# Matmul operands stored as pairs of 64-byte pieces, and activations shifted by 128 bytes

## The reference, cut to what matters

```python
def swiglu(x, wi, wo):
    gate, up = jnp.split(x @ wi, 2, axis=-1)      # wi 1024 x 5632
    return (jax.nn.silu(gate) * up) @ wo          # wo 2816 x 1024
...
for li in range(DEPTH):                           # DEPTH = 2
    h = h + 0.5 * swiglu(rms_norm(h, ffn1_norm[li]), ffn1_wi[li], ffn1_wo[li])
    hn = rms_norm(h, mix_norm[li])
    mix = gla_pool_mixer(hn, ...) if li % 2 == 0 else dsa_mixer(hn, ...)
    h = h + mix
    h = h + 0.5 * swiglu(rms_norm(h, ffn2_norm[li]), ffn2_wi[li], ffn2_wo[li])
```

## Time and profile before

| what | value |
|---|---|
| median of 2 runs | 1460.0 us (1459.95 to 1460.05) |
| the profiled execution's own time | 1459.98 us |
| its span, first to last instruction | 1458.1 us |
| PE busy | 1451.5 us, 7822 matmuls |
| DVE busy, ACT busy | 1002.2 us (69%), 777.7 us (53%) |
| moved from memory | 183 GB/s on average |
| TensorE clock granted | 1.0 throughout |

### The profile page before, as it was taken

One profiled execution on the slowest core, in us unless ns is written; L12 is line 12 of the kernel. 1 busy time (PEld: TensorE's weight loads), 2 busy tenths in 40 slices (PEclk: granted clock), 3 DMA queues, 4 the chain that ended last, 5 costly groups with the idle time before them and its releaser, 6 DMA issues.

```text
span 1458.1 us, 18627 instructions
## 1 busy us (share of the span) xinstructions
PE 1451.5 (100%) x7822; PEld 1250.3 (86%) x7822; DVE 1002.2 (69%) x1216; ACT 777.7 (53%) x971; POOL 87.1 (6%) x113
## 2 busy tenths in 40 slices
PE   9999999999999999999999999999999999999999
PEld 7888888888888888888888888888888888888887
DVE  6876466777755877459877764787646987687753
ACT  6654355655534555345665544565436876465542
POOL 0000003000000000006100000000000800000000
PEclk9999999999999999999999999999999999999999
DMA  9855563556556555545465556465556543566552
GB/s 328 277 176 185 159 204 116 167 180 201 178 184 200 190 181 195 185 141 172 149 200 188 185 177 206 154 223 182 188 173 217 188 145 118 173 196 201 179 188 72
DMA packets 205620, 266.82 MB, mean 183 GB/s; under 512 B 6944, under 2 KB 148880, under 8 KB 205280
## 3 DMA queue, kind: packets, MB, share of 16 engines
q1 hardware_dynamic: 204320, 261.23, 54.7%
q0 software_dynamic: 1072, 4.35, 0.8%
q10 hardware_dynamic: 144, 0.05, 0.0%
HBM read 264.56 MB, written 1.05 MB: 182 GB/s over the span
## 4 chain that ended last, share of the span: by engine, by line
PE 93%; DVE 3%; ACT 1%; DMA 1%; issue 0%; SPq 0%; DVEq 0%; ACTq 0%
PE ps L631 31%; PE ps L638 17%; PE ps L563 14%; PE ps L565 13%; PE ps L564 13%; PE ps L616 1%; DMA raw<-in_ffn_wi 1%; DVE wlo L1656 1%; PE ps L741 1%; PE ps L836 1%; PE ps L774 1%; DVE d_i L2049 0%; ACT whi L1217 0%; DVE d_m L2045 0%; DVE d_i L2073 0%
## 5 line engine op out<-in xcount | busy, mean ns | idle before, releaser
L1656 DVE TENSOR_TENSOR wlo<-raw,whi 128x2048 fp32r<-128x2048 f32 (+5 forms) x275 | 567.3, 2068 | 259.1 <-ACT whi L1217 258.9
L1217 ACT CAST whi<-raw 128x2048 fp32r<-128x2048 f32 (+5 forms) x275 | 474.0, 1729 | 223.0 <-PE ps L565 218.5
L631 PE MATMUL ps<-xt,whi 128*128 128x512 f32 x2112 | 501.7, 391 | 0.8 <-DVE xt L2249 0.7
L631 PEld LDWEIGHTS ps<-xt,whi 128*128 128x128 f32 x2112 | 389.3, 188 | 78.0 <-DVE xt L2249 1.5
L638 PEld LDWEIGHTS ps<-xt,wlo 128*128 128x128 f32 x2112 | 267.1, 191 | 8.2
L638 PE MATMUL ps<-xt,wlo 128*128 128x256 f32 x2112 | 269.6, 283 | 0.0
L563 PE MATMUL ps<-whi,xt 128*128 128x512 f32 (+4 forms) x304 | 112.7, 371 | 0.0
L565 PE MATMUL ps<-whi,xt 128*128 128x512 f32 (+4 forms) x304 | 109.7, 361 | 0.0
L564 PE MATMUL ps<-wlo,xt 128*128 128x512 f32 (+4 forms) x304 | 109.5, 360 | 0.0
L563 PEld LDWEIGHTS ps<-whi,xt 128*128 128x128 f32 x304 | 57.3, 189 | 9.2 <-issue 1.0
L565 PEld LDWEIGHTS ps<-whi,xt 128*128 128x128 f32 x304 | 57.2, 188 | 8.5
(11 more groups left out here) (422 smaller groups left out, 1884.3 us busy)
## 6 DMA issues: line engine op xcount, KB each, us to landing
raw<-in_ffn_wi SPq DMA_DIRECT2D x85, 1024.0 KB, 5.0
raw<-in_ffn_wo SPq DMA_DIRECT2D x40, 1024.0 KB, 4.9
raw<-in_ffn_w_gate SPq DMA_DIRECT2D x22, 1024.0 KB, 5.1
raw<-in_ffn_w_up SPq DMA_DIRECT2D x22, 1024.0 KB, 5.1
raw<-in_ffn_w_down SPq DMA_DIRECT2D x20, 1024.0 KB, 4.9
raw<-in_w_in SPq DMA_DIRECT2D x14, 1024.0 KB, 5.1
raw<-in_even_w_in SPq DMA_DIRECT2D x6, 1024.0 KB, 5.2
raw<-in_ffn_wo SPq DMA_DIRECT2D x8, 512.0 KB, 3.8
```

The costliest lines, as they stand in the source:

```text
L631: return e.matmul(Pair(job.name).ap[:, b, :], whi[:, v % SPLIT, 256 * j + 128 * b:256 * j + 128 * b + 128], XS[:, j, :, :].rearrange("p h ...
L1217: e.copy(whi[0:n, v % SPLIT, c], raw[0:n, v % RAW, c]).then_inc(s_hi.mark(*[(v, j) for j in js]), 1)
L1656: e.tensor_tensor(wlo[0:n, v % SPLIT, c], raw[0:n, v % RAW, c], whi[0:n, v % SPLIT, c].bitcast(F32), ALU.subtract).then_inc(s_lo.mark(*[(v ...
```

## The change

**Moving operands in pairs of pieces.** A moving row is no longer stored in the order in which it is read. The place it lies in is cut into two halves (for `xt` the 256 elements of the first and of the second 1024 bytes of a row of 512, for a weight block the first and second 4096 bytes of its slot), and the row is read as 16 elements (64 bytes) from the first half, 16 from the second, the next 16 from the first, and so on. The matmul's moving operand becomes a pattern of three dimensions, while its result still goes to PSUM as one unbroken row. The producers (ACT's casts, DVE's subtractions) write in the same pattern, from sources in plain order. This holds for all 4224 matmuls of `wide` and `two_wide`, and for all of `steps` and `by_tiles` but the 144 whose width is no multiple of 32 (272, 324, 360): 6954 of 7098 F32R matmuls in all, 4674 with 512 columns and 2280 with 256. Stationary operands stay unbroken.

**A shift of 128 bytes.** `xt`, `yt` and `ht` get 32 elements more. Their data now starts at an odd multiple of 128 bytes (`xt` at byte 107648, `yt` at 124032, `a1ht` at 164224), while `whi` and `wlo` stay at multiples of 256.

```diff
+class Paired(Turned):
+    def __init__(self, XS):
+        self.XS = XS
+    def moving(self, kt, q0, q1):
+        return self.XS[:, kt, :].rearrange("p (h q i) -> p q h i", h=2, i=16)[:, q0:q1]
+    def parts(self, kt, n):
+        return self.moving(kt, 0, 8)[0:n], self.moving(kt, 8, 16)[0:n]
+    def same(self, ap):
+        return ap.rearrange("p (q h i) -> p q h i", h=2, i=16)
...
-        self.hT = Turned(sb(self.name + "ht_hi", [128, 22, 256], F32R), sb(self.name + "ht_lo", [128, 22, 256], F32R))
+        room = sb(self.name + "ht", [128, 2 * 22 * 256 + 32], F32R)[:, 32:].rearrange("p (h k t) -> p h k t", h=2, k=22)
+        self.hT = Turned(room[:, 0], room[:, 1])
...
-        XS = sb("xt", [128, 8, 2, 256], F32R)
-        XT = Turned(XS[:, :, 0, :], XS[:, :, 1, :])
-        YT = Turned(sb("yt_hi", [128, 8, 256], F32R), sb("yt_lo", [128, 8, 256], F32R))
+        XS = sb("xt", [128, 4096 + 32], F32R)[:, 32:].rearrange("p (k t) -> p k t", k=8)
+        XT = Turned(XS[:, :, 0:256], XS[:, :, 256:512])
+        XP = Paired(XS)
+        yt_room = sb("yt", [128, 4096 + 32], F32R)[:, 0:4096].rearrange("p (h k t) -> p h k t", h=2, k=8)
+        YT = Turned(yt_room[:, 0], yt_room[:, 1])
...
+        def kept(w, v, n, a, b):
+            job, i = plan[v]
+            if job.blocks[0][1] == 8 or job.width % 32:
+                return w[0:n, v % SPLIT, a:b]
+            return w[0:n, v % SPLIT, :].rearrange("p (h q i) -> p q h i", h=2, i=16)[:, a // 32:b // 32]
+        def as_kept(ap, v):
+            ...
+            return ap.rearrange("p (q h i) -> p q h i", h=2, i=16)
...
-                    hi_w, lo_w = (w[0:n, v % SPLIT, j * wd:(j + 1) * wd] for w in (whi, wlo))
+                    hi_w, lo_w = (kept(w, v, n, j * wd, (j + 1) * wd) for w in (whi, wlo))
...
-                                    XS[:, j, :, :].rearrange("p h t -> p (h t)"), start=j == 0, stop=stop)
+                                    XP.moving(j, 0, 16), start=j == 0, stop=stop)
...
-                                    XS[:, j, 0, :], start=False, stop=stop)
+                                    XP.moving(j, 0, 8), start=False, stop=stop)
...
-                e.copy(whi[0:n, v % SPLIT, c], raw[0:n, v % RAW, c]).then_inc(s_hi.mark(*[(v, j) for j in js]), 1)
+                e.copy(kept(whi, v, n, c.start, c.stop), as_kept(raw[0:n, v % RAW, c], v)).then_inc(s_hi.mark(*[(v, j) for j in js]), 1)
...
-                e.tensor_tensor(wlo[0:n, v % SPLIT, c], raw[0:n, v % RAW, c], whi[0:n, v % SPLIT, c].bitcast(F32),
+                e.tensor_tensor(kept(wlo, v, n, c.start, c.stop), as_kept(raw[0:n, v % RAW, c], v), kept(whi, v, n, c.start, c.stop).bitcast(F32),
...
+                        elif act is XP:
+                            for r in range(2):
+                                if r:
+                                    t.then_inc(s_dve.mark(), 1)
+                                t = e.scalar_tensor_tensor(l[:, :, r, :], src[:, :, r, :], gains(i)[0:n, :], h[:, :, r, :].bitcast(F32), ALU.mult, ALU.subtract)
```

More of the change, by code:

```diff
@@ L137, in __init__, with parts, same @@
         self.hi, self.lo = hi, lo
+    def parts(self, kt, n):
+        return self.hi[0:n, kt, :], self.lo[0:n, kt, :]
+    def same(self, ap):
+        return ap
+class Paired(Turned):
[3 more added lines that the diff above has]
+        return self.XS[:, kt, :].rearrange("p (h q i) -> p q h i", h=2, i=16)[:, q0:q1]
+    def parts(self, kt, n):
+        return self.moving(kt, 0, 8)[0:n], self.moving(kt, 8, 16)[0:n]
+    def same(self, ap):
+        return ap.rearrange("p (q h i) -> p q h i", h=2, i=16)
 class Job:
@@ L249, in program @@
         wi1, wo1, wi2, wo2 = (T[n] for n in ("ffn1_wi", "ffn1_wo", "ffn2_wi", "ffn2_wo"))
-        a1 = Ffn("a1", "in", wi1[0], 0, wi1[0], FF, wo1[0], XT)
-        a2 = Ffn("a2", "gla", wi2[0], 0, wi2[0], FF, wo2[0], XT)
-        b1 = Ffn("b1", "a2", wi1[1], 0, wi1[1], FF, wo1[1], XT)
-        b2 = Ffn("b2", "dsa", wi2[1], 0, wi2[1], FF, wo2[1], XT)
-        c1 = Ffn("c1", "b2", T["ffn1_w_gate_2"][0], 0, T["ffn1_w_up_2"][0], 0, T["ffn1_w_down_2"][0], XT)
-        c2 = Ffn("c2", "mla", T["ffn2_w_gate_2"][0], 0, T["ffn2_w_up_2"][0], 0, T["ffn2_w_down_2"][0], XT)
+        a1 = Ffn("a1", "in", wi1[0], 0, wi1[0], FF, wo1[0],XP)
+        a2 = Ffn("a2", "gla", wi2[0], 0, wi2[0], FF, wo2[0],XP)
+        b1 = Ffn("b1", "a2", wi1[1], 0, wi1[1], FF, wo1[1],XP)
+        b2 = Ffn("b2", "dsa", wi2[1], 0, wi2[1], FF, wo2[1],XP)
+        c1 = Ffn("c1", "b2", T["ffn1_w_gate_2"][0], 0, T["ffn1_w_up_2"][0], 0, T["ffn1_w_down_2"][0],XP)
+        c2 = Ffn("c2", "mla", T["ffn2_w_gate_2"][0], 0, T["ffn2_w_up_2"][0], 0, T["ffn2_w_down_2"][0],XP)
         ga, gk, gu, gv, gg = col_jobs("gla", T["even_w_in"][0], D,
@@ L597, in by_tiles @@
                         q.wait_ge(*s_lo[v, j])
-                        hi_w, lo_w = (w[:, v % SPLIT, j * wd:(j + 1) * wd] for w in (whi, wlo))
+                        hi_w, lo_w = (kept(w, v, 128, j * wd, (j + 1) * wd) for w in (whi, wlo))
                         h, l = (a[:, kt, 128 * tt:128 * tt + 128] for a in (job.act.hi, job.act.lo))
@@ L1229, in turned @@
                         n = rows[i]
-                        t = e.mul(act.hi[0:n, kt0 + i, :], pair.flat[0:n, 256 * i:256 * i + 256], 1.0 if gains is None else gains(i)[0:n, :])
+                        t = e.mul(act.parts(kt0 + i, n)[0], act.same(pair.flat[0:n, 256 * i:256 * i + 256]), 1.0 if gains is None else gains(i)[0:n, :])
                     t.then_inc(s_act.mark((name, "hi", b)), 1)
@@ L1234, in turn_x @@
                 q.wait_ge(*s_dve["gains"])
-                turned(("xt", x, n), XT, 4 * n, lambda i: gains_of[x](4 * n + i))
+                turned(("xt", x, n), XT if x in ("a1", "b1", "c1") else XP, 4 * n, lambda i: gains_of[x](4 * n + i))
             def squares(x, n):
@@ L1613, in x_high @@
                 q.wait_ge(*s_xt[min(j // 2, 2)]["x"])
-                e.mul(XT.hi[:, j, :], XR[:, j, :], gain("f1", j)).then_inc(s_act.mark(("x0", j)), 1)
+                e.mul(XP.parts(j, 128)[0], XP.same(XR[:, j, :]), gain("f1", j)).then_inc(s_act.mark(("x0", j)), 1)
             x_high(0)
@@ L1665, in turned @@
                         n = rows[i]
-                        src, h, l = pair.flat[0:n, 256 * i:256 * i + 256], act.hi[0:n, kt0 + i, :], act.lo[0:n, kt0 + i, :]
+                        src, (h, l) = act.same(pair.flat[0:n, 256 * i:256 * i + 256]), act.parts(kt0 + i, n)
                         if gains is None:
                             t = e.tensor_tensor(l, src, h.bitcast(F32), ALU.subtract)
+                        elif act is XP:
[3 more added lines that the diff above has]
+                                t = e.scalar_tensor_tensor(l[:, :, r, :], src[:, :, r, :], gains(i)[0:n, :], h[:, :, r, :].bitcast(F32), ALU.mult, ALU.subtract)
                         else:
@@ L1673, in turn_x @@
             def turn_x(x, n):
-                turned(("xt", x, n), ("xt", x), XT, 4 * n, lambda i: gains_of[x](4 * n + i))
+                turned(("xt", x, n), ("xt", x), XT if x in ("a1", "b1", "c1") else XP, 4 * n, lambda i: gains_of[x](4 * n + i))
             def rsqrt(src, n, scales, *outs):
@@ L2248, in x_low @@
                 q.wait_ge(*s_act["x0", j])
-                e.scalar_tensor_tensor(XT.lo[:, j, :], XR[:, j, :], gain("f1", j), XT.hi[:, j, :].bitcast(F32),
-                                       ALU.mult, ALU.subtract).then_inc(s_dve.mark((("xt", "in"), j)), 1)
+                h, l = XP.parts(j, 128)
+                x = XP.same(XR[:, j, :])
+                for r in range(2):
+                    e.scalar_tensor_tensor(l[:, :, r, :], x[:, :, r, :], gain("f1", j), h[:, :, r, :].bitcast(F32),
+                                           ALU.mult, ALU.subtract).then_inc(s_dve.mark(*([(("xt", "in"), j)] if r else [])), 1)
             x_low(0)
```

2 lines of the change are left out of this document (1 added, 1 removed).

## The result

The changed kernel takes **1517.15 us** (1517.09 to 1517.22) where the kernel before takes 1460.0: ratio 1.0391, 95% interval 1.0374 to 1.0408. It is 57 us slower, and the forecast was 1389 us with a range to 1463.

What follows compares the result with a forecast made beforehand. PE's F32R start-to-start pace was taken as the bound. Gains of 25.3, 28.2 and 24.4 us (256 columns) made 77.9, times 0.93 gives 72.4; 1460 - 72.4 + 1 for DVE gave 1389 us, range up to 1463.

Steps and rivals of the forecast that it cites:

- What bounds the kernel: Whole kernel: the pace at which PE starts F32R matmuls sets the time; PE is 93% of the chain of waits.
- Is it a conflict of two reads?: F32R matmuls: moving read loses some 13 ns to the next weights' load in the same memory part; the change separates them.
- a floor of 215.5 ns: 512-column matmuls: pace expected after the change, from float32 records at 215 ns, in place of 227.5 or 226.5.
- the two terms of the 512-column matmuls: 2112 matmuls in gate and up were to gain 25.3 us, the other 2562 were to gain 28.2 us.
- 13 ns that don't grow with its columns: F32R matmuls of 256 and 512 columns: each carries some 13 ns extra, whose shared companion is one LDWEIGHTS of 128 columns.
- The float32 records at 215 ns: Plain float32 matmuls of 256 columns: at half the reading pace, with the same LDWEIGHTS, the 13 ns shrink to 2.
- The 360-column rows at 160 and 165 ns: 360-column job: extra of 10 ns at one offset and 15 at others, read as a cost that depends on address.
- The rule of two read ports: Skill page, TensorE: loading weights takes no read bandwidth from the running matmul, so no conflict to remove; time would stay.
- Rival 2: F32R matmuls: streams keep pace while meeting, 1550 us, or jumps cost one step each, 1537 us; slower cases 0.18.
- Casts and subtractions in pieces at no cost: 225 ACT casts and 225 DVE subtractions writing 64-byte pieces: taken at nothing, with 7% as bound.
- 48 more DVE instructions for about 1 us: Splits on DVE: 10 us of DVE time, nearly all beside PE; 1 us taken, bounds 0 and 3.
- 7% of the chain is not PE: Start and mixer stretches: a faster PE waits longer there, so 77.9 us of gain counts as 72.4.

Runs made afterwards that it cites:

- pieces_alone: The changed kernel with its pieces of 16 elements kept and the shift of 128 bytes taken out: 1517.29 us in one execution.
- pieces_256: The changed kernel with pieces of 64 elements (256 B) in place of 16 and no shift: 1460.0 us, ratio 0.9999 to the kernel before.

## Why the prediction was wrong, step by step

**What bounds the kernel** held: the time followed PE's pace, with a chain of 99% PE.

**The step that failed is "Is it a conflict of two reads?"** It took the 13 ns for a clash of the moving read with the next weights' load, and everything after it (a floor of 215.5 ns, 12 ns gained on 512 columns, 10.7 on 256) hangs on that; and what a jump costs PE's own reading stands in the sum at nothing. The runs showed that the 13 ns stay with 8 columns to load in place of 128, and that a piece of 64 B costs two steps. So the two terms of the 512-column matmuls, forecast as 25.3 and 28.2 us less, measured 24.7 and 31.8 us more, and the 24.4 us less of the 256-column ones measured 1.0 more. The evidence was read too far at three points:
- *"13 ns that don't grow with its columns."* The same 13 ns at 256 and 512 columns looked like something common to each matmul, the load. With 32 columns to load, rows of 128, 256 and 512 carry 16, 27 and 44 steps: it grows. And shrinking the load to 32, 8 or 1 columns takes nothing off a row of 512, and 3 ns at most off one of 256.
- *The float32 records at 215 ns.* That a slower reader loses only 2 ns speaks for any limit on float32r's fetch, not for the load as its cause. bf16 rows, with a 128-column load beside them (of half the bytes), take 215.8 too.
- *The 360-column rows at 160 and 165 ns.* The place does matter, but it is another effect, of 6.7 ns at 512 columns, that comes with a distance of the operands other than a multiple of 256 B, and lies on top of the 13. The first packed row starts at 0 modulo 256 B, the others at 160, 64 and 224 (1440 B apart). The kernel before had the good distance already in all but the 144 matmuls of odd widths; the change's shift of 128 B took it away. A part of the evidence *for* the change was a sign of what the change would break. The distance isn't the whole account of these rows, though: in pieces_alone, where the first packed row and what is loaded beside it lie as before, it takes 0.98/6 = 163 ns in place of 160. Why it does is open.

**The rule of two read ports** (the Trainium skill, "TensorE: Matmul & The Clock Gate", Part 2, step 1) came out closer than the reading of the trace. It says that loading the next weights takes no read bandwidth from the running matmul. The runs agree with it as far as the load's size at 512 columns goes: with 1 to 96 columns to load a row takes 226.7 to 231.7 ns, never less than the 226.7 of 128. They differ where the stationary operand's place counts, since moving it alone by 64 or 128 B takes the same row to 233 ns, and at 256 columns, where 8 columns to load give 116.7 ns and 128 give 120.0; there the measurement decides.

**The rivals.** Rival 2 gave, as its second half, "a jump every 16 elements could cost the same by itself", with one step per piece, 240 ns for 512 columns and 1537 us. The 240 ns are exact, the cause (the jumps) is the one shown, and "it decides at half a step per jump" was passed. That the figure is exact is in part luck: it added one step per jump to the plain row's own extra, while the runs have two steps per piece in place of that extra, and the two come to the same at 512 columns alone. So its size was 20 us too high: it charged 6.7 ns to each of the 2280 matmuls of 256 columns (15 us), and these pay nothing, because what a plain row of 256 takes over its columns already covers two steps for each of its 16 pieces; the other 5 us are 512-column matmuls that were slower than the best pace before. Its first half (the two streams meeting and keeping pace) is refuted: with 512 columns pieces of 16 take 240.0 ns at every distance and load that was run. The range ended at 1463, since both its halves were among the slower cases with 0.18. For a read pattern that no row of the trace showed, that was too little: the one row used against it, ACT's pieces, is of another engine, and the prediction itself noted that it reads at a lower pace.

**Part by part.** Casts and subtractions in pieces at no cost: held (1905 and 2301 ns), though the prediction counted 225 of each and only 99 write in pieces. 48 more DVE instructions for about 1 us: held, pieces_256 has them and takes 1460.0. A split at 343 ns a half: measured 343. The odd widths, taken at nothing: 0.1 us more over all 144. "7% of the chain is not PE" was turned into a factor of 0.93 on the gain. No run made PE faster by as much, so the factor stays untested; but the chain's share is no measure of slack. It rose to 99% although what PE's 512-column distances have over 250 ns shrank by only 0.5 us: the stretches of other engines that the chain before held ran beside a PE that was hardly less busy.

**What stays open.** Why a plain float32r row takes 544 steps for 512 columns where a bf16 row takes 518. The load's size, the PSUM side (one bank or an output in pieces leave 226.7) and the place (one and the same moving row each time leaves 226.7) don't explain it. Also why pieces of 12 or 24 elements cost less than those of 16, and why the distance modulo 256 B counts when a smaller load doesn't help: with 32 columns to load the row takes 230.7 to 232 ns at every distance.

## What to carry to other kernels

A matmul's extra over its columns is not known to be the load's until a row with a smaller load has shown it; forty matmuls of one form in a row answer that in a single run. A read pattern that no row of the trace has deserves a price of its own, and a chance for it, before it is put at nothing. float32r moving operands should be read in runs of at least 256 B, and the moving and stationary tiles should start at the same place modulo 256 B (in the whole kernel, pieces of 256 B and a shift of 256 B were both free to 0.1%). Where three products make up one float32 product, the correction terms are candidates for bf16: one of the two, in five of six layers' gate and up, gave 1.0% here.

## What the runs showed of the hardware that was not expected

- Float32r moving reads in pieces of 64 B take 9/8 of the columns: 240.0 ns for 512, 180.0 for 384, 120.0 for 256. With 512 columns, pieces of 128 B take 236.7 ns, of 256 B 226.7, of 16 B 250. bf16 rows in pieces of 32 or 64 B don't pay it (215.8).
- Every second float32r element takes 451 ns for 512 columns; pieces of 64 B displaced by 8 B take 300.
- A distance of the two operands other than a multiple of 256 B takes a row of 512 from 226.7 to up to 233.3 ns, and one of 128 B takes this kernel from 1460 to 1480.7 us. A displacement by 256 B leaves it at 1459.96.
- Less to load isn't faster at 512 columns: a plain row takes 231.7 ns with 32 columns to load and 226.7 with 128. At 256 columns it is, a little: 116.7 ns with 8 and 120.0 with 128.
- Over its columns a bf16 row takes 6 steps of 2.4 GHz at 128, 256 and 512 columns; a float32r row with 32 columns to load takes 16, 27 and 44.
